# A hybrid decoder block: the down weights of expert block 28 in memory of their own

## The reference

```
h   = [meta tokens (16); x (256)]                       # 272 x 1024, float32
h   = h + token_mixer(rmsnorm(h))                       # gated convolution beside 4-head retention
xn  = rmsnorm(h); logits = xn @ w_router + b_router     # 32 experts
gates, experts = softmax(top 4 of logits)
for every block of tokens of one expert e:
    hgu = xb @ w_gate_up[e] + b_gate_up[e]              # 1024 -> 2 x 1024
    act = min(gate, 7) * sigmoid(1.702 * gate) * (clip(up, -7, 7) + 1)
    y   = act @ w_down[e] + b_down[e]                   # 1024 -> 1024
    h[token] += gate_of_token * y
out = rmsnorm(h)[16:]                                   # 256 x 1024
```

## Time and profile before

| | |
|---|---|
| median of three runs | 1316.84 us |
| the profiled execution | 1317.12 us, of it a span of 1315.4 us |
| PE busy | 1257.4 us, 96% |
| DVE, ACT busy | 574.1 us (44%), 291.6 us (22%) |
| moved by DMA | 467.48 MB |
| mean granted TensorE clock | 0.997 |

### The profile page before, as it was taken

How to read it: one execution, slowest core, us unless ns; L and a number is a source line. 1 busy time by engine, 2 the same in 40 slices (tenths; PEclk the granted TensorE clock), 3 DMA queues, 4 the chain that set the end, 5 groups by cost and what they waited for, 6 DMA issues and landing times.

```text
span 1315.4 us, 21204 instructions
## 1 busy us (share of the span) xinstructions
PE 1257.4 (96%) x8579; PEld 716.9 (55%) x8579; DVE 574.1 (44%) x1109; ACT 291.6 (22%) x510; POOL 15.1 (1%) x38
## 2 busy tenths in 40 slices
PE   8999999999999999998999999999999989999997
PEld 8999889999983343333333333334333333343332
DVE  6898899987646232322232222223222222222231
ACT  5453444445451111110110011001100110011111
POOL 2000000000000000000000000000000000000000
PEclk9999999999999999999999999999999999999999
DMA  9744453457788999999999999999999999999995
GB/s 319 241 161 139 137 172 128 152 169 228 272 356 328 420 430 430 430 430 428 432 431 432 432 432 433 432 431 430 430 430 431 432 432 431 432 431 425 428 428 221
DMA packets 77901, 467.48 MB, mean 355 GB/s; under 512 B 4391, under 2 KB 62295, under 8 KB 63303
## 3 DMA queue, kind: packets, MB, share of 16 engines
q1 hardware_dynamic: 77863, 466.95, 86.8%
HBM read 465.89 MB, written 1.05 MB: 355 GB/s over the span
## 4 chain that ended last, share of the span: by engine, by line
PE 65%; DMA 32%; DVE 2%; issue 1%; ACT 0%; DVEq 0%; SPq 0%; ACTq 0%
PE pb L825 18%; PE pb L581 18%; PE pb L852 10%; DMA work<-in_w_gate_up 7%; DMA work<-in_w_down 7%; DMA late_w<-in_w_gate_up 5%; DMA split_w<-in_w_gate_up 5%; DMA late_w<-in_w_down 4%; DMA split_w<-in_w_down 4%; PE pb L882 3%; PE pb L740 2%; PE pb L771 2%; PE pb L666 1%; PE pb L668 1%; PE pb L667 1%; PE pb L545 1%
## 5 line engine op out<-in xcount | busy, mean ns | idle before, releaser
L1663 DVE TENSOR_SCALAR work<-pb 64x512 f32<-64x512 f32 x64 | 43.7, 683 | 527.0 <-PE pb L832 525.8
L825 PE MATMUL pb<-work,ubuf 128*64 128x512 f32 x992 | 220.3, 597 | 19.8 <-DMA work<-in_w_gate_up 19.8
L581 PE MATMUL pb<-parts,whi 128*128 128x272 f32 (+1 forms) x1280 | 174.6, 287 | 0.1
L581 PEld LDWEIGHTS pb<-parts,whi 128*128 128x128 f32 x1280 | 163.1, 189 | 3.8 <-issue 3.4
L825 PEld LDWEIGHTS pb<-work,ubuf 128*64 128x64 f32 x992 | 74.3, 138 | 152.6 <-issue 152.4
L1215 DVE TENSOR_TENSOR wlo<-work,whi 128x1024 fp32r<-128x1024 f32 x104 | 126.4, 1222 | 34.7 <-ACT whi L984 34.4
L825 PE MATMUL pb<-late_w,ubuf 128*64 128x512 f32 x576 | 127.0, 593 | 9.2 <-DMA late_w<-in_w_gate_up 9.2
L984 ACT ACTIVATE whi<-work 128x1024 fp32r<-128x1024 f32 x104 | 109.9, 1060 | 112.8 <-PE pb L581 87.4
L852 PE MATMUL pb<-work,ubuf 128*64 128x512 f32 x576 | 131.2, 597 | 2.7 <-DMA work<-in_w_down 1.2
L825 PE MATMUL pb<-split_w,ubuf 128*64 128x512 f32 x472 | 104.1, 593 | 10.0 <-DMA split_w<-in_w_gate_up 9.6
L1150 ACT ACTIVATE work<-work 64x512 f32<-64x512 f32 x64 | 39.9, 624 | 281.7 <-DVE work L1663 281.7
(11 more groups left out here) (249 smaller groups left out, 1242.6 us busy)
## 6 DMA issues: line engine op xcount, KB each, us to landing
work<-in_w_gate_up SPq DMA_DIRECT2D x28, 4096.0 KB, 30.8
split_w<-in_w_gate_up SPq DMA_DIRECT2D x14, 4096.0 KB, 30.8
late_w<-in_w_gate_up SPq DMA_DIRECT2D x13, 4096.0 KB, 30.8
work<-in_w_down SPq DMA_DIRECT2D x12, 4096.0 KB, 29.0
work<-in_w_in SPq DMA_DIRECT2D x39, 1024.0 KB, 5.1
late_w<-in_w_down SPq DMA_DIRECT2D x7, 4096.0 KB, 29.0
split_w<-in_w_down SPq DMA_DIRECT2D x7, 4096.0 KB, 29.0
work<-in_w_down SPq DMA_DIRECT2D x11, 2048.0 KB, 18.5
```

The lines of the kernel that those rows point to most:

```text
L581: ins = pe.matmul(pb[:, bank + j, 0:TALL - t0], w[:, x, k * UNIT + j * P:k * UNIT + (j + 1) * P], of[:, c * KC // 2 + k, t0:TALL], start=( ...
L825: ins = pe.matmul(pb[u * SLOTS:(u + 1) * SLOTS, bank, :], xT[:, 2 * i + k, :], w[:, k, u * HID:(u + 1) * HID], start=(i == 0 and k == 0), ...
L1663: dve.tensor_scalar(hg, pb[0:SLOTS, 4 + s, :], LIMIT, None, ALU.min).then_inc(min_rdy, 1)
```

## The change

`FIXED` becomes 29, so block 28 belongs to the blocks with a fixed expert. It is written out behind the loop of six passes and in front of `add_residual`. Its down unit (unit 87) is not loaded through the places: its four megabytes go to `kept`, which is cv, the two halves of a new tensor `spare` of 16 KB per partition, and hw. The room for `spare` comes from the dynamic-DMA scratch, set to 1 KB. `spare` is loaded between the gate columns of w_in, cv where `extra` was loaded, and hw at the start of the block loop, as soon as the tokens are gathered and the third part is made (gathered, xr_rdy); for this, DVE makes the third part inside `further_blocks`, behind the counts of blocks. Unit 4 lies wholly in places 0 to 3 and is loaded in parts of 1, 1 and 2 MB. The dynamic blocks are 29 and 30 now, and their 12 places are 12 to 15 and 0 to 7 (`later_place`).

```diff
@@ -41,7 +41,7 @@
 LOADS = 12
 AHEAD = 4
 PLACES = 16
-FIXED = 28
+FIXED = 29
 HW = KC * UNIT // 2
 HS = 4
 Y3 = KC * REAL + 256
@@ -129,6 +129,7 @@
         slotc = sb("slotc", [P, TT])
         bst = sb("bst", [P, TT, 6])
         bmv = sb("bmv", [P, TT, 4])
+        spare = sb("spare", [P, 4 * D])

         upad = ubuf[:, :].rearrange("p (a b) -> p a b", a=KC)

@@ -218,7 +219,8 @@
         xn2T = flat[:, 0:KC * REAL].rearrange("p (a b) -> p a b", a=KC)
         osb = rflat[:, KC * REAL:2 * KC * REAL].rearrange("p (a b) -> p a b", a=TT)
         nwb = rflat[:, 4096:5120]
-        extra = cv[:, :, :].rearrange("p a b -> p (a b)")
+        kept = [cv[:, :, :].rearrange("p a b -> p (a b)"), spare[:, 0:2 * D], spare[:, 2 * D:4 * D],
+                hw[:, :, :].rearrange("p a b -> p (a b)")]

         x_in, meta_in, wmb_in = [sem(f"x_in{t}") for t in range(TT)], sem("meta_in"), sem("wmb_in")
...
@@ -317,6 +319,10 @@
             first = n_scratch - 4 * D + (n - 8) * 2 * D
             return work[:, first:first + count * 2 * D]

+        def later_place(n, count=1):
+
+            return place_at(4 * (3, 0, 1)[n // 4] + n % 4, count)
+
         ROW2 = P // 2

         block = ctx.enter_context(nc.Block())
@@ -343,20 +349,24 @@
                 x = e + (b + 1 if i % 3 == 2 else b) if i else 0
                 sp.dma_start(place_at(4 * (i % 4), 4), expert_src(x, of, q)).then_inc(e_in[i % 4], 16)

-            def pair_of_four(i, e, half):
+            def part_of_four(i, first, n):

                 b = (i - 1) // 3
                 of, q = ((w_dn, 0), (w_gu, 1), (w_gu, 0))[i % 3]
-                x = e + (b + 1 if i % 3 == 2 else b)
-                sp.dma_start(place_at(4 * (i % 4) + 2 * half, 2),
-                             expert_src(x, of, q)[:, half * 4 * D:(half + 1) * 4 * D]).then_inc(e_in[i % 4], 16)
+                x = b + 1 if i % 3 == 2 else b
+                sp.dma_start(place_at(4 * (i % 4) + first, n),
+                             expert_src(x, of, q)[:, first * 2 * D:(first + n) * 2 * D]).then_inc(e_in[i % 4], 16)
+
+            def keep(to, first, n, done):
+
+                sp.dma_start(to, expert_src(FIXED - 1, w_dn, 0)[:, first * 2 * D:(first + n) * 2 * D]).then_inc(done, 16)

             def used(i):

                 return 4 * i + 4

             def later_pair(n, e, of, i):
-                sp.dma_start(place_at(AHEAD + n, 2), expert_src(e, of, i // 4)[:, i % 4 * 2 * D:(i % 4 + 2) * 2 * D]).then_inc(l_in[n // 2], 16)
+                sp.dma_start(later_place(n, 2), expert_src(e, of, i // 4)[:, i % 4 * 2 * D:(i % 4 + 2) * 2 * D]).then_inc(l_in[n // 2], 16)

             xr = a["x"][0].rearrange("(t p) n -> p t n", p=P)
             for t in range(TT):
@@ -398,6 +408,8 @@
             for g in range(UC):
                 load(GATE0 + 2 * g, w_in, U_GA + g)
                 load(GATE0 + 2 * g + 1, w_in, U_GB + g)
+                if g == 1:
+                    keep(spare[:, :], 1, 2, kept_in[1])
             for r in range(UC):
                 load(LRET + 2 * r, w_ro[:, 0:KC, :], r)
                 load(LRET + 2 * r + 1, w_ro[:, KC:2 * KC, :], r)
@@ -420,27 +432,32 @@
             four(0, 0)
             sp.dma_start(wr, a["w_router"][0].rearrange("(k p) n -> p k n", p=P)).then_inc(rout_in, 16)
             sp.dma_start(brb, a["b_router"][0:1, :].to_broadcast([P, NE])).then_inc(rout_in, 16)
-            sp.dma_start(extra, expert_src(1, w_gu, 1)[:, 0:2 * D]).then_inc(first_in[0], 16)
+            keep(kept[0], 0, 1, kept_in[0])

             sp.wait_ge(merged, KC)
             four(2, 0)
             for half in range(2):
                 sp.wait_ge(mix_done, 6 + 2 * half)
-                pair_of_four(3, 0, half)
+                part_of_four(3, 2 * half, 2)
             sp.wait_ge(xr_rdy, 2)
             sp.dma_start(nwb, a["norm_final_w"].rearrange("(o n) -> o n", o=1)[0:1, :]
                          .to_broadcast([P, D])).then_inc(nwb_in, 16)

-            fours = 3 * FIXED + 1
+            fours = 3 * FIXED
             trips = (fours - 8) // 12
             sp.wait_ge(w_used, 1)
-            sp.dma_start(place_at(0), expert_src(1, w_gu, 1)[:, 2 * D:4 * D]).then_inc(first_in[1], 16)
-            sp.wait_ge(w_used, 3)
-            sp.dma_start(place_at(1, 2), expert_src(1, w_gu, 1)[:, 4 * D:8 * D]).then_inc(e_in[0], 16)
+            part_of_four(4, 0, 1)
+            sp.wait_ge(gathered, 1)
+            sp.wait_ge(xr_rdy, 4)
+            keep(kept[3], 3, 1, kept_in[2])
+            sp.wait_ge(w_used, 2)
+            part_of_four(4, 1, 1)
+            sp.wait_ge(w_used, 4)
+            part_of_four(4, 2, 2)
             for i in range(5, 7):
                 for half in range(2):
                     sp.wait_ge(w_used, used(i - 4) - 2 + 2 * half)
-                    pair_of_four(i, 0, half)
+                    part_of_four(i, 2 * half, 2)
             sp.wait_ge(w_used, used(3))
             four(7, 0)
             with sp.Fori(0, trips) as g:
...
@@ -776,15 +793,11 @@

                 def at(n):
                     i, part = 3 * j + 1 + n // 4, n % 4
-                    if i % 4 == 0:
-                        if i == 4 and part < 2 and isinstance(g, int):
-                            pe.wait_ge(first_in[part], 16)
-                        else:
-                            pe.wait_ge(e_in[0], 48 * g + 16 * (i // 4 + 1))
-                        if i == 4 and isinstance(g, int):
-                            return place_at(part - 1) if part else extra
-                    else:
-                        pe.wait_ge(e_in[i % 4], 48 * g + (16 if i < 3 else 32 if i == 3 else 16 * (i // 4 + 2)))
+                    if isinstance(g, int) and 12 * g + i == 3 * FIXED:
+                        pe.wait_ge(kept_in[(0, 1, 1, 2)[part]], 16)
+                        return kept[part]
+                    parts_before = 2 if i % 4 == 0 else 0 if i < 3 else 1
+                    pe.wait_ge(e_in[i % 4], 48 * g + 16 * (i // 4 + 1 + parts_before))
                     return place_at(4 * (i % 4) + part)
                 return at

...
@@ -937,6 +950,7 @@
             with pe.Fori(0, FIXED // 4 - 1) as g:
                 for j in range(4):
                     whole(4 * g + (4 + j), fixed_unit(g, 4 + j))
+            whole(FIXED - 1, fixed_unit(FIXED // 4 - 1, 4))
             add_residual()
             with pe.Fori(0, rounds) as i:
                 whole(i + FIXED, later_unit(i))
@@ -1575,6 +1589,7 @@
                 do(dve.tensor_tensor_scan(pend[:, :], ones[:, 0:NE], nblk[:, :], 0.0, ALU.mult, ALU.add))
                 dve.tensor_scalar(nblocks[:, 1:2], pend[0:1, NE - 1:NE], float(NE - 1), None, ALU.add).then_inc(table_done, 1)
                 dve.tensor_scalar(nblocks[:, 0:1], pend[0:1, NE - 1:NE], float(NE - 1 - FIXED), None, ALU.add).then_inc(table_done, 1)
+                third_part(1, hw[:, 1, :], 4)
                 c3 = pick[:, TT * TOPK * NE:TT * TOPK * NE + n_more * NE].rearrange("p (b e) -> p b e", e=NE)
                 do(dve.tensor_tensor(c3, pend[:, :].rearrange("p (o e) -> p o e", o=1).to_broadcast([P, n_more, NE]),
                                      iota_b[:, 0:n_more].rearrange("p (b o) -> p b o", o=1).to_broadcast([P, n_more, NE]),
@@ -1620,7 +1635,6 @@
                 dve.tensor_tensor(part, part, fnw(4 * half, 4 * half + 4), ALU.mult).then_inc(xt_rdy if half else xh_rdy, 1)
             rest_of(1, hw[:, 1, :], 3)
             further_blocks()
-            third_part(1, hw[:, 1, :], 4)
             for t in range(TT):
                 dve.wait_ge(exp_done, t + 1)
                 do(dve.reciprocal(stat[:, 12 + t:13 + t], stat[:, 10 + t:11 + t]))
@@ -1736,7 +1750,7 @@
     import concourse.bacc as bacc
     from concourse.bass_utils import run_bass_kernel_spmd as run

-    nc = bacc.Bacc("TRN2", target_bir_lowering=False, num_devices=1)
+    nc = bacc.Bacc("TRN2", target_bir_lowering=False, num_devices=1, dynamic_dma_scratch_size=1024)
     arrays, aps = {}, {}
     tables = shape_tables()
     tables.update(expert_units(np.asarray(inputs["w_gate_up"]), np.asarray(inputs["w_down"])))
```

More of the change, by code:

```diff
@@ L228, in build_block @@
         e_in = [sem(f"e_in{s}") for s in range(PLACES // 4)]
-        first_in = [sem(f"first_in{i}") for i in range(2)]
+        kept_in = [sem(f"kept_in{i}") for i in range(3)]
         end_in = [sem(f"end_in{i}") for i in range(2)]
@@ L477, in _ @@
             for i in range(2):
-                sp.dma_start(place_at(AHEAD + 6 + i), expert_src(el, w_dn, 0)[:, (2 + i) * 2 * D:(3 + i) * 2 * D]).then_inc(end_in[i], 16)
+                sp.dma_start(later_place(6 + i), expert_src(el, w_dn, 0)[:, (2 + i) * 2 * D:(3 + i) * 2 * D]).then_inc(end_in[i], 16)
             outr = out[0].rearrange("(t p) n -> p t n", p=P)
@@ L794, in at @@
                     pe.wait_ge(l_in[n // 2], 16 * i + 16)
-                    return place_at(AHEAD + n)
+                    return later_place(n)
                 return at
```

## The result

The changed kernel takes 1318.67 us (median of 20 executions, 1317.81 to 1320.70), the kernel before, timed beside it, 1316.38 (20, 1315.71 to 1317.76): ratio 1.0019, 95% interval 1.0013 to 1.0025. It is slower by about 2.3 us, on the edge of the 0.2% that the forecast called no change. The profiled execution took 1319.41 us, its span is 1317.6.

The account below looks back on a forecast made before the run. PE was taken to bound the kernel up to about block 6 and from block 28, weights through blocks 7 to 27. Loop 0, residual and break +0.7, front 0, code 0 gave 1317.6 us, range 1315.4 to 1320.2.

Parts of the forecast that it names:

- Points 1 and 6: Block 28's down unit leaves the loop's stream: gain 0. No part is numbered 6; the scratch appears only in Rival D.
- Rival A: End of the run: DMA ends it, so 4 MB less shorten it by 9.7 us, to 1307.1; chance 0.12.
- Rival D: Dynamic-DMA scratch: the smaller scratch throttles the queue, giving over 1400 us; chance 0.02.
- Points 3 to 5: Reloading after block 28: cost 0; loads moved to the front: 0 to +0.1; block 28 written out: 0, up to +0.9.
- rival C: Front, 396 to 418: 2 MB more are not absorbed and delay landings up to block 28, +4.9 to 1322.5; chance 0.06.
- Point 2: Block 28 of whole units, ahead of the residual: PE waits for weights landing at 1202.0; about +0.7 us.
- Sum: +0.6 +0.15: Block 29 begins at 1232.6 instead of 1232.00, then takes 26.78 instead of 26.63 after a break; about +0.7 us.
- Rival B: Block 28's start: the granted clock falls after PE's idle time, unhidden, +1.7 to 1319.3, with late fetch 1320.2; chance 0.14.

Follow-up runs that it names:

- run 6: Changed kernel keeping block 24's down unit instead of block 28's, blocks 24 to 28 written out, residual ahead of block 28: 1308.17 us, ratio 0.9946 to before.
- run 7: As run 6, with the residual moved behind block 3: 1307.41 us, ratio 0.9933 to the kernel before.
- run 3: Kernel before's blocks with only the changed front, small scratch and moved loads, kept pieces loaded but not read: 1316.86 us, ratio 1.0001 to before.
- run 1: Changed kernel with the residual moved back ahead of block 28: 1315.86 us, ratio 0.9994 to the kernel before.
- run 9: The changed kernel itself, unedited, timed again in a later call: 1318.78 us, ratio 1.0018 to the kernel before.
- run 5: Changed kernel with the residual moved from behind block 28 to behind block 3: 1316.03 us, ratio 0.9995 to the kernel before.

## Why the prediction was right, and where its sum was off

The class (no change within 0.2%) and the range hold; the forecast of 1317.6 was 1.1 us too low, and its difference to before, +0.7, was a third of the measured +2.3. The median lies 0.2 us above the forecast's own range (1316.5 to 1318.5).

*Points 1 and 6, the unit and the scratch.* The gain of 0 behind the last wait was right: the loads end 5.9 us earlier (10 were said) and nobody waits for them. Runs 6 and 7 show that it is the place that made it 0. Rival A did not come true for this unit; that run 7, with another unit, lies 0.3 us from its 1307.1 is luck in part, since that run has the residual moved as well. Rival D, the throttle, is ruled out by run 3.

*Points 3 to 5, reloading, front and code.* Cost 0, as run 3 (1.0001) shows for the front and run 1 (0.9994) for reloading and code, which run 3 does not have; rival C is ruled out. Two steps on the way were wrong without a price. The queue did run dry behind block 28 (DMA share 0.83 from 1215 to 1220), but no wait for a DMA follows block 28. And the halves issued from 418.05 landed 2.5 us later, not within 0.2; the last one, at 432.7, came just ahead of the 433 from which on the text saw rival C decided, so the cost of 0 had less to spare than the text thought.

*Point 2, block 28 of whole units.* The mechanism was the right one, step by step: landing at 1201.75 for 1202.0, a wait of 2.0 us (the text said under 2), and, in the execution without a fall (run 9), the residual at 1228.73 for 1228.9 and block 29 at 1232.36 for 1232.6. The mis-sized step is the comparison, "Sum: +0.6 +0.15", where the medians moved by 2.3 us. It set a forecast without a fall of the clock beside a profile of before in which one, at 1173.05, had cost 1.7 us that reached the end. Like set against like, by spans of profiled executions:

| | a fall that reaches the end | none |
|---|---|---|
| residual ahead of block 28 (with: before; without: run 1) | span 1315.4 | span 1313.7 |
| residual behind it (with: after; without: run 9) | span 1317.6 | span 1315.9 |

The difference is 2.2 us in either column. It is the residual's 3.63 us, which lie behind the wait now, less the 1.67 of them that block 28 begins earlier (1201.88 for run 1's 1203.55), plus 0.2 for block 29's start behind a break and rounding. The text saw the pieces: it wrote that a fall "at the same place would vanish in the wait for 1202.0". By that, a sum for executions without a fall should have been made from 1203.5 (1205.22 less the 1.7 that it had in hand), where run 1 begins block 28 (1203.55), not from 1205.22.

This account is shown for the changed kernel and for run 1, not for the kernel before, of which there is one profile only. Run 1's loads behind block 28 have the early stream of the change. Run 3, with the blocks of before and their unit in the stream (and 4 MB more at the front), had no fall at 1173.70 and still took a span of 1315.9, because its weights were later and block 30 waited 1.1 us for them. How much the kernel before gains in an execution without a fall stays open. What the times themselves say: run 9's profiled execution lies 0.6 us above the one of before (1317.72, 1317.12), as the +0.7 forecast for it; the other 1.7 of the measured 2.3 us is that the median of before lies 0.7 under its profiled execution, and the median of the changed kernel 1.0 above that of run 9.

*Rival B* is what the profiled execution of after did (1319.3 forecast, 1319.41 measured). As a rival to the forecast it was misnamed: the changed kernel has executions with the fall and without it (run 9), and the one profile of before has a fall too, so it tells executions of one kernel apart, not the two kernels. The median of 1318.67 lies between the prices of B and of the forecast.

## What to carry to other kernels

Work that can stand anywhere (here 3.63 us of additions into the accumulators) is best put in front of the last wait for data, or earlier (runs 1 and 5 take the same time); before moving a block past it, look for what covers that wait. A load taken out of a saturated stream paid here only where waits for that stream would have followed it: run 6 used the same memory four blocks earlier and, beside run 1, turned -0.6 us into -7.8. And before a profiled row becomes the base of a sum, ask whether it carries a fall of the clock that not every execution has.

## What the runs showed of the hardware

- The same program with the same idle time of TensorE (2.01 and 2.02 us ahead of 1201.88) ran its next 32 matmuls in 8.78 us in one execution, with the granted clock at 0.81 on the mean of the stretch, and in 7.09 in another, at 1.00.
- 4 MB issued near 429.2 landed after 13.5 us (442.7) when the load ahead of it had landed at 432.7, and after 13.7 us (443.0) when that one had landed at 430.2; 4 MB units that follow one another in a full queue land 9.7 us apart. So 2 MB more ahead of it did not move it.
